# First feed-forward layer in the seven-product form, its modulation jobs spread over block pairs and output chunks

## What is computed

```python
for l in range(DEPTH):                       # DEPTH = 2
    m  = (silu(c)     @ w_mod[l] + b_mod[l]) # 9 modulation vectors for latent tokens
    mc = (silu(c_ctx) @ w_mod[l] + b_mod[l]) # and 9 for context tokens
    h = h + 0.5 * m[2] * swiglu(modulate(h, m[0], m[1]), w_ff1_in[l], w_ff1_out[l])
    ...                                      # the same for the context
    h = h + m[5] * mixer(modulate(h, m[3], m[4]))
    h = h + 0.5 * m[8] * swiglu(modulate(h, m[6], m[7]), w_ff2_in[l], w_ff2_out[l])

def swiglu(t, w_in, w_out):
    gate, up = split(t @ w_in, 2)
    return (silu(gate) * up) @ w_out
```

## Time and profile before

| | us |
|---|---|
| three runs | 3272.66, 3274.56, 3278.45 (median 3274.56) |
| the profiled execution | 3272.6, its span 3270.8 |
| TensorE busy in the span | 3102.8 (95%), 17735 products |
| VectorE busy | 1938.7 (59%) |
| ScalarE busy | 1110.4 (34%) |
| GpSimd busy | 266.0 (8%) |

### The profile page before, as it was taken

One profiled execution on the slowest core, in us unless ns is written; L12 is line 12 of the kernel. 1 busy time (PEld: TensorE's weight loads), 2 busy tenths in 40 slices (PEclk: granted clock), 3 DMA queues, 4 the chain that ended last, 5 costly groups with the idle time before them and its releaser, 6 DMA issues.

```text
span 3270.8 us, 43730 instructions
## 1 busy us (share of the span) xinstructions
PE 3102.8 (95%) x17735; PEld 2739.3 (84%) x17735; DVE 1938.7 (59%) x2755; ACT 1110.4 (34%) x1734; POOL 266.0 (8%) x317
## 2 busy tenths in 40 slices
PE   5999999999999998898999999999999998999999
PEld 4999999987669895488999988999998876678887
DVE  7754536524552536757778765877778548643333
ACT  4211212356441321235323334532323436632222
POOL 1100000200001005620000001000000100000000
PEclk8999999999999999999999999999999999999999
DMA  6533424411004220012343321333333120023332
GB/s 209 169 102 108 124 72 137 127 36 52 7 1 129 59 64 14 1 39 70 112 129 104 116 65 59 110 97 102 111 116 110 56 61 8 14 83 97 96 97 90
DMA packets 314304, 274.20 MB, mean 84 GB/s; under 512 B 17426, under 2 KB 290057, under 8 KB 313865
## 3 DMA queue, kind: packets, MB, share of 16 engines
q1 hardware_dynamic: 286992, 182.35, 18.7%
q0 software_dynamic: 25488, 89.14, 8.7%
q10 hardware_dynamic: 1641, 0.14, 0.0%
HBM read 263.21 MB, written 8.39 MB: 83 GB/s over the span
## 4 chain that ended last, share of the span: by engine, by line
PE 50%; DVE 4%; ACT 2%; issue 1%; POOL 0%; ACTq 0%; DVEq 0%
PE ps L2236 28%; PE ps L497 16%; PE ps L1453 1%; DVE hs_lo L2437 1%; ACT gpt L1492 1%; DVE vw_lo L2169 1%; ACT gp L1505 1%; PE ps L1211 1%; PE ps L1477 1%; PE ps L1435 1%; PE ps L2318 0%; DVE ms_s L2468 0%; DVE h_sb L2445 0%; PE ps L1891 0%; PE ps L1908 0%
## 5 line engine op out<-in xcount | busy, mean ns | idle before, releaser
L487 DVE TENSOR_TENSOR w_lo<-ring,w_hi 128x1024 fp32r<-128x1024 f32 (+3 forms) x221 | 251.4, 1139 | 450.2 <-ACT w_hi L472 361.7
L497 PE MATMUL ps<-u_hi,w_hi 128*128 128x384 f32 (+2 forms) x1584 | 469.1, 356 | 19.6 <-DVE u_lo L663 15.4
L497 PE MATMUL ps<-u_lo,w_hi 128*128 128x384 f32 (+2 forms) x1584 | 461.9, 351 | 0.0
L497 PE MATMUL ps<-u_hi,w_lo 128*128 128x384 f32 (+2 forms) x1584 | 461.5, 351 | 0.0
L472 ACT CAST w_hi<-ring 128x1024 fp32r<-128x1024 f32 (+3 forms) x157 | 149.4, 952 | 612.3 <-PE ps L497 574.1
L497 PEld LDWEIGHTS ps<-u_hi,w_hi 128*128 128x128 f32 x1584 | 284.9, 190 | 47.9 <-issue 23.2
L497 PEld LDWEIGHTS ps<-u_lo,w_hi 128*128 128x128 f32 x1584 | 286.4, 190 | 22.7 <-issue 1.7
L2169 DVE TENSOR_TENSOR vw_lo<-ring,vw_hi 128x1024 fp32r<-128x1024 f32 (+1 forms) x176 | 211.2, 1200 | 155.6 <-ACT vw_hi L2163 155.3
L497 PEld LDWEIGHTS ps<-u_hi,w_lo 128*128 128x128 f32 x1584 | 285.4, 189 | 21.2
L2163 ACT CAST vw_hi<-ring 128x1024 fp32r<-128x1024 f32 (+1 forms) x176 | 181.3, 1030 | 330.5 <-PE ps L2236 267.4
L2236 PE MATMUL ps<-u_hi,vw_hi 128*128 128x384 f32 x768 | 249.0, 338 | 11.8 <-DVE u_lo L663 10.9
(11 more groups left out here) (350 smaller groups left out, 5854.8 us busy)
## 6 DMA issues: line engine op xcount, KB each, us to landing
ring<-in_w_ff_in SPq DMA_DIRECT2D x176, 512.0 KB, 4.0
ring<-in_w_ff_out SPq DMA_DIRECT2D x72, 512.0 KB, 4.0
cst<-in_w_mod POOLq DMA_DIRECT2D x72, 512.0 KB, 3.9
m_in<-in_w_mod POOLq DMA_DIRECT2D x56, 512.0 KB, 4.0
ring<-in_w_in_e SPq DMA_DIRECT2D x26, 512.0 KB, 3.9
m_first<-in_w_mod POOLq DMA_DIRECT2D x16, 512.0 KB, 13.9
ring<-in_w_out_e SPq DMA_DIRECT2D x16, 512.0 KB, 3.8
ring<-in_w_ff_out SPq DMA_DIRECT2D x16, 384.0 KB, 3.4
```

The lines of the kernel that those rows point to most:

```text
L487: dve.tensor_tensor(w_lo[:, b:b + WIDE[n]], ring[:, s:s + WIDE[n]], w_hi[:, b:b + WIDE[n]], ALU.subtract).then_inc(w_split_lo, 1)
L497: mm = pe.matmul(ps_at(p, c0, c1) if halved else pair(p)[:, c0:c1], w, x[:, c0:c1], start=start and i == 0, stop=stop and i == 2)
```

## The change

Layer 0 joins the seven-product form (`STR = (0, 1, 2)`), with all that goes with it: parts of `SPART`, its sums and mixes, its pieces in the constants' space. `MODS_AT` is empty: all seven jobs are finished inside the layer. The layout of items changes. In layer 0 the P chunks and pair 1 hold a list of their own (`urgent`), 17 items, so that the first job is done at the first output chunk; other pairs hold 2, 2, 1 and 1 items in A chunks 2, 3, 4 and 6. In all three layers a job's result now follows in the same chunk as TensorE's products, two chunks behind the fold, and as `busy` is cleared there, the next job's items start in that chunk. The constants are loaded again after layer 0 as well, with waits of TensorE, VectorE and GpSimd before their next use.

```diff
-STR = (1, 2)
+STR = (0, 1, 2)
...
-        MODS_AT = {1: (0, 2)}
-        SEAM_BANKS = {1: (4, 5)}
+        MODS_AT = {}
+        SEAM_BANKS = {}
...
-            plan, c = {}, 0
+            plan = {}
             busy = -1
+            urgent = {("P", 0, 0): 3, ("P", 0, 1): 3, ("P", 0, 2): 2, ("P", 0, 3): 1, ("A", 1, 0): 1, ("A", 1, 1): 1,
+                      ("A", 1, 2): 1, ("A", 1, 3): 2, ("A", 1, 4): 2, ("A", 1, 5): 1} if i_f == 0 else {}
+            usual = {2: 2, 3: 2, 4: 1, 6: 1} if i_f == 0 else {2: 1, 3: 2, 4: 1}
             for c, ch in enumerate(S_ORDER[i_f]):
-                cap = {2: 1, 3: 2, 4: 1}.get(ch[2], 0) if ch[0] == "A" else 3
-                if ch[0] == "P":
-                    cap = 0
+                cap = 3 if ch[0] == "O" else usual.get(ch[2], 0) if ch[0] == "A" else 0
+                if urgent and ch[0] != "O" and ch[1] < 2:
+                    cap = urgent.get(ch, 0)
                 plan[c] = {"dve": [], "pe": []}
                 if busy >= 0 and c == busy + 2:
                     plan[c]["pe"].append(done)
-                if busy >= 0 and c == busy + 3:
                     plan[c]["dve"].append(("d", done))
                     busy = -1
                 while cap > 0 and todo and busy < 0:
...
                         dve_s_prod(dve, i_f, 0, 1, 1)
+                    for x in items:
+                        dve_s_mod_item(dve, i_f, x)
                     continue
...
-            sync_ff(f, 0)
+            sync_s(f, 0)
...
-            pe_ff(pe, 0)
+            pe_s_ff(pe, 0)
             pe_norm(pe, 1)
+            pe.wait_ge(const_back, 16)
...
-                act_split(act, BASE[NEXT[0]] + c)
+                act_s_split(act, 0, c)
...
-            act_ff(act, 0)
+            act_s_ff(act, 0)
...
-                dve_split(dve, BASE[NEXT[0]] + c)
+                dve_s_split(dve, 0, c)
...
-            dve_ff(dve, 0)
+            dve_s_ff(dve, 0)
             dve_norm(dve, 1)
+            dve.wait_ge(const_back, 16)
...
-            for part in PARTS:
-                pool_mod(pool, 0, part)
+            pool_s_mod(pool, 0)
             pool_squares(pool, 1)
             pool_keep(pool)
             pool_fetch(pool)
+            pool.wait_ge(const_back, 16)
```

More of the change, by code:

```diff
@@ L2124, in s_wait_buffer @@
             else:
-                back_to_back = i_f - 1 in STR and i_f > 1
+                back_to_back = i_f == 2 and 1 in STR
                 if back_to_back:
@@ L2745, in _ @@
             pe_norm(pe, 4)
-            pe.wait_ge(const_back, 16)
+            pe.wait_ge(const_back, 32)
             pe_items(pe, n_even, len(items), 4)
@@ L2876, in _ @@
             dve_norm(dve, 4)
-            dve.wait_ge(const_back, 16)
+            dve.wait_ge(const_back, 32)
             dve_items(dve, n_even, len(items))
```

## The result

The changed kernel takes 3290.63 us (median of five runs, 3288.05 to 3296.29) against 3274.56 before: ratio 1.0050, interval 1.0035 to 1.0064. It is 16 us slower where 3272.6 and "within 0.2%" were forecast, and it lies above the range. The profiled execution took 3290.63, its span 3288.8.

The account below looks back on a forecast made before the run. TensorE's product count bounds plain layer 0; the change trades products for VectorE work. Layer 0 -6.9, seam -0.2 and later layers +5.1 give -2.0 us in the profiled execution, forecast median 3272.6; 8-in-10 range 3256 to 3286.

Parts of the forecast that it names:

- Products removed, three more jobs: Layer 0: 240 products go, 41.6 us bare gain; three more jobs' small products on TensorE cost 1.88 us each, +5.6.
- The clock behind a job: Layer 0: products behind 3 of 7 jobs take 1.54 us more, where layer 1 had 1; +3.1 (0 to +7).
- The first pairs, +7.8: Layer 0, pairs 0 and 1: VectorE's added items delay TensorE, +7.8 net; bounds +2.4 and +11.
- +8.3: Layer 0's first pairs: cost before subtracting 0.5 for the wait before the first output; TensorE's restart moves by 7.2.
- The item in the last chunk, +3.5 and +1.6: Layer 0's usual pairs: low half awaited 1.2 us at five outputs, +3.5; VectorE late into four following pairs, +1.6.
- Pieces: Layer 0: transfer landing of 4.0 us counted for chunk 0's items only; pieces not landed were put at nothing.
- The seam, -0.2: Seam behind layer 0: the norm's own steps set it, 9.23 us instead of 9.42.
- The later layers, +5.1: Layers 1 and 2: the new placement rule puts folds into output chunks; +5.1 together, bounds 0 and +7.
- The four waits: Layers 1 and 2, third and fourth parts: a fold in an output chunk delays a residual, 4 x 1.2 = +4.8.
- the late adds: Layer 0: after a pair with a last-chunk item VectorE is late, reaching TensorE as 0.4 in four pairs, +1.6.
- The second rival: Layer 0: VectorE becomes the bound, each last-chunk item delaying the next pair's sums 1.2 us, +14 in all, 3286; 20%.
- The first rival: Layer 0 and later layers: VectorE absorbs the added work in its idle time, -12.7 more, 3260; 25%.

Follow-up runs that it names:

- e7: Changed kernel with the items of layer 0's first job on 16 of 1024 columns from the second block on; 3279.67 us, one run.
- e1: Changed kernel with the last squares and residuals ahead of the weight splits in the norm behind layer 0; 3284.44 us, 1.0031 to the kernel before the change.
- e2: Changed kernel with items of layer 0's later jobs held back so every pair begins with a whole piece; 3283.57 us, 1.0037 to the kernel before the change.
- e3: Changed kernel with the old placement rule (a job's result one chunk later) in layers 1 and 2; 3281.95 us, 1.0028 to the kernel before the change.
- e5: Changed kernel with seam squares first, layer 0's items held back and the old placement rule in layers 1 and 2; 3268.80 us, 0.9983 to the kernel before.
- e10: Kernel with all three repairs, plus a usual pair's sixth item in layer 0 moved from last to fourth chunk; 3278.70 us, 1.0016 to the kernel before.
- e9: Changed kernel with only layer 0's first two pieces fetched and read again by all items; 3280.29 us, 1.0025 to the kernel before the change.
- e8: Kernel before the change with only the new placement rule (a job's result one chunk earlier); 3281.09 us, 1.0019 to the kernel before.
- after: The changed kernel itself, against the kernel before the change; 3290.63 us, ratio 1.0050.
- e4: Changed kernel with layer 0's items of pieces 1 to 7 working on 16 of 1024 columns; 3258.86 us, one run.
- e6: Kernel with all three repairs, plus each job's 32 small products spread between large ones; 3276.06 us, 1.0003 to the kernel before the change.

## Why the prediction was wrong

Three steps of the prediction failed, besides smaller ones. A term for the lower clock was given to jobs only and not to waits for VectorE. The pieces' landing was put at nothing behind the first ones. And the seam was put at -0.2, as if the norm's own steps set it. The runs showed wider spacing of +9.3 us beyond the forecast in layer 0, 6.6 us of waits of TensorE that hang on the pieces, and +5.7 in the seam in their place. Point by point, in the order of its sum:

- **Products removed, three more jobs.** As counted: 240 fewer, 1.88 us a job.
- **The clock behind a job.** Forecast 3 of 7, seen 4 of 7 at 1.56. The size of one and nearly the count were right. The step that failed is that only jobs were given such a term. The clock also falls behind waits for VectorE: 3.6 us in the first pairs (between 98 and 115), 1.8 behind the residual that was awaited until 513.84 and 1.8 behind the add that was awaited until 581.88. It doesn't do so behind all of them: the waits of 1.39, 1.83 and 3.11 us until 392.04, 423.29 and 550.07 were followed by the full clock. With the restart steps layer 0 paid 12.4 more than layer 1 before, where 3.1 was allowed; this is the largest single miss, 9.3 us, of which 3.6 lie in the first pairs, whose sum had been put down as waits.
- **The first pairs, +7.8.** The same stretch takes 68.3 us in layer 1 before; with +8.3 it would be 76.6, and it took 76.7. e7 shows the mechanism. The gaps are 5.1 and not 7.2 longer, and the clock fills the difference. In the five other profiles with the same code there (e1, e2, e3, e5, e10) the gaps are 5.0 to 7.7 longer, while the stretch stays at 76.6 to 77.1: VectorE's work sets its length, and what the lower clock takes here comes out of the gaps.
- **The item in the last chunk, +3.5 and +1.6.** The low halves are awaited 0.68 us instead of 1.2: +0.2 each, where 0.7 was forecast. An item of 1.2 us that costs 0.2 must have found more slack ahead of the pair's last product than the 0.46 that was read from the trace before. The waits behind such pairs, 0.41 and 0.42, are what was forecast.
- **Pieces.** "If something waits that I have at nothing (pieces not landed ...)" stood among what would make it wrong, and it did. I took the landing time of 4.0 us for the first pieces and never asked it for the others. With five items in three neighbouring chunks instead of four, a pair that begins with a piece half used wants its fourth item 3.4 us after the request, and the piece took 4.6 to 5.9. 8.7 us of waits of VectorE, 6.6 us of TensorE (e9), 8 to 9 with the clock.
- **The seam, -0.2.** The sentence was that the norm's own steps set it, on the ground that the seam behind another seven-product layer took 9.23. But that seam leads to a stage whose first weights take the other place. The change put `old_place` into the first seam, and ScalarE's queue was not followed through it. +5.7 (e1).
- **The later layers, +5.1.** The four waits came as forecast, 4.4 us for 4.8. All waits of the two layers grew by 4.8 us and the stretches at the lower clock by 3.5, together 8.3 (8.1 in e8).

By size, against the forecast of -2.0 in the profiled execution and +18.0 seen: the wider spacing, mostly the clock, +9.3 in layer 0 and some 3 in the later layers, the late adds +7.9 (9.5 where 1.6 was forecast, the pieces behind nearly all of it), the seam +5.9; against it the outputs -2.9, the gaps of the first pairs -2.7 (the other side of the clock's 3.6 there), and -1.9 outside all this. Some 1.4 are not accounted for.

The second rival, VectorE as the bound (3286), came nearest in time, but not by its mechanism: no pair delays the next in full, and after the repairs in e5 VectorE is as busy as in after (454.2 us) and the kernel 22 us faster. The first rival, that VectorE absorbs it, is refuted by e4 and e7.

What stays open is why the clock falls behind some jobs and not behind others. Several microseconds of layer 0's length, between three profiles of the same code, go with it.

## What to carry to other kernels

When more work is moved onto a helper engine, follow its inputs as well as its time: with two buffers, two items a piece and 4 to 6 us from issue to landing, four items in quick succession got through when the first found a piece whole; a fourth behind a half used piece (after) and a fifth (e10) had to wait. A stage that is brought into another's form inherits all of its seams: follow each in-order queue through the new one, above all a strict wait that stands ahead of short work on the critical path. And where the array's clock can fall, price a new wait of TensorE at more than its own length: here 4.8 us more of waits in the later layers came with 8.3 us.

## What the runs showed of the hardware

A product of 512 + 256 columns has two spacings in one and the same part. In e5, from TensorE's timeline:

```profile
143.30 0.51 PE L2252 MATMUL ps<-hs_hi,vw_hi 128*128 128x512 f32 x2
155.44 0.51 PE L2252 MATMUL ps<-hs_hi,vw_lo 128*128 128x512 f32 x2
156.05 0.59 PE L2252 MATMUL ps<-hs_hi,vw_hi 128*128 128x512 f32 x2
156.47 0.51 PE L2252 MATMUL ps<-hs_lo,vw_hi 128*128 128x512 f32 x2
169.90 0.51 PE L2252 MATMUL ps<-hs_hi,vw_hi 128*128 128x512 f32 x2
```

From 143.30 to 155.44 there are 70 at 0.1734 us, from 156.47 to 169.90 76 at 0.1767, and between them a step of 0.33 us that no semaphore explains. The 0.1787 of the forecast was read from a stretch at the higher spacing with two such steps in it (0.10 and 0.18 us, at 1565.65 and 1579.18 in the trace before); by the timeline its 174 output products took 0.1783 each. The Trainium skill (TensorE: Matmul & The Clock Gate, Back-to-back issue gap) gives an isolated product's spacing by its columns alone, one figure for both stretches, and says itself that in a stream the weight loads count too; the forecast took it for the stream. The trace has two figures.

Small products between large ones cost 2.53 us a job (e6) instead of 1.88 when all 32 stand together.
